# Output projection as seven products of half-size blocks instead of eight, with some of its sums of weights made by accumulating DMAs

## The chip, the core and the metric

One NeuronCore of a Trainium2 chip runs the whole layer. The metric is the device time of one execution in microseconds (us). The engines are TensorE (PE, its weight loads PEld), VectorE (DVE), ScalarE (ACT), GpSimd (POOL) and SyncE (SP), which issues nearly all DMAs.

## What is computed

A decoder layer for 512 tokens of width 2048 in float32: norm, one input projection, three groups of attention heads (16 heads of width 128), a gate, one output projection, a norm, and the residual. The part that matters here:

```
        y = jnp.concatenate([merge_heads(out_a) * jax.nn.silu(ga),
                             merge_heads(out_b) * jax.nn.silu(gb),
                             merge_heads(out_m) * jax.nn.silu(gm)], axis=-1)
        o = jnp.einsum('bse,ed->bsd', y, w_out[layer])
        x = x + rms_norm(o, g_post[layer])
```

y is 512 x 2048, w_out is 2048 x 2048, and the result o is 512 x 2048.

## The kernel before

Every float32 matrix is split into a high part that TensorE takes exactly (float32r) and a low remainder. ACT writes the high part (`hi`, line 859), DVE subtracts it from the original for the low part (`minus`, line 1208), and `three` (lines 540 to 542) issues three matmuls: high x high, low x high, high x low.

**Input projection.** `product(p, i)` works on 28 pairs of column strips. Each pair is done in seven products TOK_A to TOK_G instead of eight, by sums and differences of the halves of tokens and weights (Strassen's way in Winograd's form). Four of the seven take a sum of two weight pieces, added on DVE (line 1237); the split operands go through a ring of three slots, so ACT and DVE work three products ahead of TensorE. The results are combined by small copies and additions in PSUM and SBUF (lines 951, 955, 959, 1325, 1328).

**Output projection.** `out_block(c, p, s)` is plain: for four chunks c of 512 columns, eight pieces p of 256 rows of w_out and four blocks s of 128 tokens, two times three matmuls of 128x128 by 128x512. That is 4 x 8 x 4 x 2 x 3 = 768 matmuls. Eight split buffers hold a whole chunk of w_out, four PSUM banks collect one chunk while the other four are read. y lies in DRAM (`y_dram`), is loaded back by `load_y` one head at a time, and is split by `split_y` (ACT, line 1148) and `lo_y` (DVE). The last head's attention is finished in between: `turn_v`, `turn_probs` and `prob_times_v` (line 688) stand behind pieces 0, 1 and 3 of chunk 0. After each chunk ACT squares and copies its four banks (lines 1178, 1180) and DVE multiplies by the gain g_post (`gpost`, line 1587). In the last chunk the blocks of tokens end one after the other. Each is closed by a root on ACT (line 901), four small DVE steps, four multiply-adds with the residual (line 1611) and four stores (line 529).

**What sets the order.** Every engine has its own queue, written out by hand, with waits on counting semaphores. SP's queue holds all loads in order, so a wait in front of one load holds up every load behind it; `gpost` (line 520) is loaded once the whole of y is split. POOL issues no DMA.

## Time and profile before

| | us |
|---|---|
| median of 3 runs | 936.09 (935.10 to 938.37) |
| profiled execution, its own time | 936.1 |
| its span in the profile | 934.3 |
| end of the input projection on TensorE | 741.65 |
| first matmul of the output projection | 746.48 |
| TensorE, share of the span busy | 97% |
| DVE / ACT, share of the span busy | 70% / 51% |

The time of an execution is 1.8 us more than the span. Start times in the profile are counted from the start of the span. An instruction's duration overlaps its neighbours' a little, so the distance between two starts, and not the duration, tells how fast an engine gets through a row of like instructions.

### The profile page before, as it was taken

How to read it: one execution, taken by the hardware profiler on the slowest of the kernel's cores; microseconds unless marked ns; L12 is line 12 of the kernel's file. 1: busy time of each engine (PE TensorE's matmuls, PEld its weight loads, DVE VectorE, ACT ScalarE, POOL GpSimd, SP SyncE). 2: the span in 40 equal slices, each digit the busy share in tenths (PEclk: the TensorE clock that was granted, in tenths of full speed). 3: DMA queues.
4: the chain of work that ended last, by engine and by line, in shares of the span. 5: the costliest groups of instructions: out<-in, count | busy, mean ns of one | idle time of the engine just before them, and what ended most of it. 6: DMA issues, size and time to landing. Idle time of an engine off the chain costs nothing.

```text
span 934.3 us, 16316 instructions
## 1 busy us (share of the span) xinstructions
PE 901.8 (97%) x6619; PEld 856.4 (92%) x6619; DVE 649.8 (70%) x940; ACT 474.3 (51%) x862; POOL 79.0 (8%) x71
## 2 busy tenths in 40 slices
PE   8997998999999999999999999999999799999996
PEld 5887998999999999999999999999999788888885
DVE  4889978888777777777777777777777653532324
ACT  5786555555545455555555554546464552541311
POOL 0000508600000000000020201011110000000000
PEclk9999999999999999999999999999999999999999
DMA  9951424343334333343434352525252717632016
GB/s 301 290 137 46 127 78 102 102 115 102 102 102 103 102 102 102 103 105 99 114 91 120 85 136 72 148 66 145 70 136 82 260 65 284 234 91 68 0 47 224
DMA packets 155312, 113.42 MB, mean 121 GB/s; under 512 B 6041, under 2 KB 137145, under 8 KB 154086
## 3 DMA queue, kind: packets, MB, share of 16 engines
q1 hardware_dynamic: 154950, 111.34, 41.9%
q8 instruction: 52, 0.85, 0.4%
q10 hardware_dynamic: 288, 1.05, 0.4%
q14 instruction: 22, 0.18, 0.1%
HBM read 104.22 MB, written 9.73 MB: 122 GB/s over the span
## 4 chain that ended last, share of the span: by engine, by line
PE 81%; DVE 10%; ACT 4%; issue 3%; DVEq 0%; POOL 0%; ACTq 0%; POOLq 0%
PE d_ps L540 12%; PE d_ps L542 12%; PE d_ps L541 12%; PE e_ps L540 6%; PE e_ps L542 6%; PE e_ps L541 6%; PE c_ps L540 3%; PE c_ps L542 3%; PE c_ps L541 3%; PE pt_ps L688 3%; DVE ring L1208 3%; PE score_ps L541 2%; PE score_ps L540 2%; PE score_ps L542 2%; DVE sums L1237 2%
## 5 line engine op out<-in xcount | busy, mean ns | idle before, releaser
L1208 DVE TENSOR_TENSOR ring<-sums,ring 128x1024 fp32r<-128x1024 f32 x112 | 140.4, 1255 | 95.7 <-ACT ring L859 95.0
L540 PE MATMUL d_ps<-tok_hi,ring 128*128 128x256 f32 x672 | 191.2, 285 | 2.9 <-DVE ring L1208 2.9
L542 PE MATMUL d_ps<-tok_lo,ring 128*128 128x256 f32 x672 | 190.1, 283 | 0.0
L541 PE MATMUL d_ps<-tok_hi,ring 128*128 128x256 f32 x672 | 190.1, 283 | 0.0
L1208 DVE TENSOR_TENSOR ring<-raw,ring 128x1024 fp32r<-128x1024 f32 x100 | 124.5, 1249 | 45.2 <-ACT ring L859 45.2
L540 PEld LDWEIGHTS d_ps<-tok_hi,ring 128*128 128x128 f32 x672 | 128.9, 192 | 3.3 <-issue 3.3
L859 ACT ACTIVATE ring<-sums 128x1024 fp32r<-128x1024 f32 x112 | 117.9, 1052 | 22.0 <-DVE sums L1237 20.4
L541 PEld LDWEIGHTS d_ps<-tok_hi,ring 128*128 128x128 f32 x672 | 129.0, 192 | 0.0
L542 PEld LDWEIGHTS d_ps<-tok_lo,ring 128*128 128x128 f32 x672 | 128.9, 192 | 0.0
L859 ACT ACTIVATE ring<-raw 128x1024 fp32r<-128x1024 f32 x100 | 105.2, 1058 | 37.5 <-PE d_ps L542 37.5
L1208 DVE TENSOR_TENSOR wout_split<-raw,wout_split 128x1024 fp32r<-128x1024 f32 x32 | 39.1, 1224 | 71.8 <-ACT wout_split L859 71.2
L1237 DVE TENSOR_TENSOR sums<-sums,raw 128x1024 f32<-128x1024 f32 x56 | 69.9, 1248 | 0.0
L1237 DVE TENSOR_TENSOR sums<-raw 128x1024 f32<-128x1024 f32 x56 | 69.8, 1246 | 0.1
L859 ACT ACTIVATE wout_split<-raw 128x1024 fp32r<-128x1024 f32 x32 | 33.8, 1061 | 69.4 <-PE e_ps L542 29.6
L540 PE MATMUL c_ps<-tok,ring 128*128 128x256 f32 x224 | 64.5, 288 | 0.1
L540 PE MATMUL e_ps<-tok_hi,ring 128*128 128x256 f32 x224 | 64.3, 287 | 0.0
L540 PE MATMUL e_ps<-tok,ring 128*128 128x256 f32 x224 | 64.3, 287 | 0.0
L542 PE MATMUL e_ps<-tok_lo,ring 128*128 128x256 f32 x224 | 63.4, 283 | 0.0
L542 PE MATMUL d_ps<-tok,ring 128*128 128x256 f32 x224 | 63.4, 283 | 0.0
L541 PE MATMUL d_ps<-tok,ring 128*128 128x256 f32 x224 | 63.4, 283 | 0.0
L542 PE MATMUL c_ps<-tok,ring 128*128 128x256 f32 x224 | 63.4, 283 | 0.0
L540 PE MATMUL d_ps<-tok,ring 128*128 128x256 f32 x224 | 63.4, 283 | 0.0
(279 smaller groups left out, 2281.0 us busy)
## 6 DMA issues: line engine op xcount, KB each, us to landing
raw<-in_w_in_dram SPq DMA_DIRECT2D x112, 512.0 KB, 5.5
raw<-in_w_out_dram SPq DMA_DIRECT2D x32, 512.0 KB, 5.6
raw<-in_w_mem_kv_dram SPq DMA_DIRECT2D x16, 512.0 KB, 8.3
stage<-in_x_dram SPq DMA_DIRECT2D x4, 1024.0 KB, 9.2
xres<-in_x_dram SPq DMA_DIRECT2D x4, 1024.0 KB, 8.3
out_dram<-o_sb SPq DMA_DIRECT2D x16, 256.0 KB, 3.3
y_dram<-ybuf SPq DMA_DIRECT2D x15, 256.0 KB, 2.3
y_f<-y_dram SPq DMA_DIRECT2D x15, 256.0 KB, 5.2
```

The lines of the kernel that those rows point to most:

```text
L540: pe.matmul(dst, lhs[0], rhs[0], start=start, stop=False, skip_group_check=True)
L541: pe.matmul(dst, lhs[1], rhs[0], start=False, stop=False, skip_group_check=True)
L542: return pe.matmul(dst, lhs[0], rhs[1], start=False, stop=stop, skip_group_check=True)
L688: last = pe.matmul(bank[:, first:S], v, pT[:, hl_p, kb, first:S] if not head.memory else pT_mem[:, hl_p, kb, first:S], start=(hl_v, hl_p, ...
L859: act.activation(dst, src, ACTF.Copy).then_inc(hi_done, 1)
L1208: return dve.tensor_tensor(dst, a_, hi_.bitcast(F32), ALU.subtract)
L1237: dve.tensor_tensor(sum_tile(p, s), one, two, ALU.add).then_inc(sum_done, 1)
```

## The change

The output projection now is done like the input projection. The columns go in two groups g of 1024, the rows of w_out and of y in two halves, the tokens in two halves of 256, and each group is seven products (g, TOK_A) to (g, TOK_G). A product is four steps j (two row tiles of 128 each), a step is 2 x 2 x 3 = 12 matmuls of 128x128 by 128x512. There are 2 x 7 x 4 = 56 steps, in the order of `STEPS`. TOK_A and TOK_D of both groups, which need no sum of weights and no sum of y, stand first as steps 0 to 15; then come B, C, E, F, G of group 0 (steps 16 to 35) and of group 1 (36 to 55).

Split weights go through the same ring of three slots of one step each. ACT and DVE run a loop over the steps: at n they split step n+3, and ACT may begin that when TensorE has done step n. Sums of weights (TOK_B, C, E, F, four pieces each and group: eight sets) are made one step earlier still on DVE (`add_out`), except for three sets, (0, B), (0, F) and (1, F), where a DMA issued by POOL adds a piece of w_out from DRAM onto a tile in SBUF (`add_piece`). y is loaded from DRAM in its quarters (`load_y`), and four sums and differences of quarters (`add_y`, 128x2048) and the splits (`hi_y`, `lo_y`, 128x2048) are spread over n = 0 to 19. PSUM results are combined in `out_taken`; the result of A in negated form is the start value ("seed") of D's banks. The gain is now applied from PSUM or from the combined tile (`gain`), with no copy; `finish` closes the blocks of tokens in the order 2, 3, 0, 1, all four behind the split of the last piece. In the last product, (1, G), the steps run once for each of its two token blocks.

```diff
+OUT_PRODUCTS = [(0, TOK_A), (0, TOK_D), (1, TOK_A), (1, TOK_D)] + [
+    (g, i) for g in range(OUT_GROUPS) for i in (TOK_B, TOK_C, TOK_E, TOK_F, TOK_G)]
+STEPS = [(g, i, j) for g, i in OUT_PRODUCTS for j in ((0, 2, 3, 1) if (g, i) == (0, TOK_D) else range(SUBS))]
+STEP_OF = {step: n for n, step in enumerate(STEPS)}
+ADDED_BY_DMA = [(0, TOK_B), (0, TOK_F), (1, TOK_F)]
...
+RAW_USES = [(g, i) for g, i in OUT_PRODUCTS
+            if i in (TOK_D, TOK_G) or (g, i) == (1, TOK_A) or i in (TOK_B, TOK_E, TOK_F) and (g, i) not in ADDED_BY_DMA]
+OUT_PART = {TOK_A: (0, 0), TOK_B: (1, 1), TOK_D: (0, 1), TOK_E: (1, 0), TOK_F: (0, 1), TOK_G: (1, 1)}
...
+            def load_piece(g, i, j):
+                use = RAW_USES.index((g, i))
+                if use == 0:
+                    sp.wait_ge(lo_done, operand(last_pair, TOK_G) + 1)
+                else:
+                    h, k = RAW_USES[use - 1]
+                    if k in (TOK_A, TOK_D, TOK_G):
+                        sp.wait_ge(lo_done, out_operand((h, k, j)) + 1)
+                    else:
+                        sp.wait_ge(sum_done, out_sum_count((h, k, j)))
+                sp.dma_start(as_rows(raw[:, j]), w_out_piece(g, *OUT_PART[i], j)).then_inc(piece_landed[j], 16)
...
+            load_piece(1, TOK_A, 0)
+            load_y(TOK_F)
+            load_piece(1, TOK_A, 2)
+            load_piece(1, TOK_A, 3)
+            load_piece(1, TOK_A, 1)
+            load_y(TOK_G)
+
+            def load_pieces(g, i):
+                if (g, i) in RAW_USES:
+                    for j in range(SUBS):
+                        load_piece(g, i, j)
+
+            for j in range(SUBS):
+                load_other(0, j)
+            load_pieces(1, TOK_D)
+            sp.wait_ge(y_raw, NH)
             sp.dma_start(gpost[:], g_post.partition_broadcast(P)[:, 0, :]).then_inc(gpost_landed, 16)
...
-            def out_block(c, p, s):
-                e0 = out_e0(p)
-                w = wout_split[p][:].rearrange("p h (j n) -> p h j n", j=2)
-                for j in range(2):
-                    tok_cols = slice(P * s, P * (s + 1))
-                    last = three(out_ps[c % 2][s][:], (y_hi[:, e0 + j, tok_cols], y_lo[:, e0 + j, tok_cols]),
-                                 (w[:, 0, j], w[:, 1, j]), p == 0 and j == 0, p == OPC - 1 and j == 1)
...
+            def out_passes(g, i, j, b, bank):
+
+                w = out_slot((g, i, j)).rearrange("p h (e n) -> p h e n", e=2)
+                hi, lo = token_operand(i)
+                cols = slice(P * b, P * (b + 1))
+                for e in range(2):
+                    k = 2 * j + e
+                    last = three(bank[b][:], (hi[:, k, cols], lo[:, k, cols]), (w[:, 0, e], w[:, 1, e]),
+                                 i in (TOK_A, TOK_B) and k == 0, k == KH - 1)
                 return last
 
...
+                if i == TOK_A and g == 1:
+                    pe.wait_ge(y_raw, NH)
+                    pe.wait_ge(v_ready, last_head.v + 1)
+                if i == TOK_B and g == 1:
+                    pe.wait_ge(o_gained, result_count(0, TOK_F, 1))
+                if i in (TOK_D, TOK_C):
+                    pe.wait_ge(out_seeded, 2 * (g + 1))
+                if i == TOK_E:
+                    pe.wait_ge(out_six_taken, 2 * (g + 1))
+                if i == TOK_F:
+                    pe.wait_ge(out_less_six, 2 * (g + 1))
+                if i == TOK_G:
+                    pe.wait_ge(out_last, 2 * (g + 1))
+
...
+                if n == 3:
+                    pe.wait_ge(pt_ready, last_head.pt + 3)
+                    for b in range(2):
+                        pe.matmul(out_c[b][:], pT[:, 0, 0, 0:P], pT[:, 0, 0], start=True, stop=True
...
+                elif (g, i) in ADDED_BY_DMA:
+                    act.wait_ge((first_added if i == TOK_E else other_added)[j], added_count(g, i))
                 else:
-                    act.wait_ge(o_done, QB * c)
-                hi(out_operand(c, p), wout_split[p][:, 0], raw_tile(m))
+                    act.wait_ge(sum_done, out_sum_count(step))
+                if step == STEPS[-1]:
+                    act.wait_ge(lo_done, out_operand((g, TOK_F, 1)) + 1)
...
-            def copy_out(c, s):
-                act.wait_ge(o_done, QB * c + s + 1)
-                bank = out_ps[c % 2][s]
-                if c + s:
-                    act.wait_ge(part_done, QB * c + s)
-                act.activation(waste_o[:], bank[:], ACTF.Square, accum_out=part[:, s:s + 1]
-                               ).then_inc(part_done, 1)
-                act.activation(o_sb[:, s, S * c:S * (c + 1)], bank[:], ACTF.Copy).then_inc(o_copied, 1)
...
+            def out_taken(g, i):
+
+                if i == TOK_A:
+                    act.wait_ge(used, product_end(g, i))
+                    if g == 0:
+                        act.wait_ge(bank_marked, 2)
+                    else:
+                        act.wait_ge(o_gained, result_count(g - 1, TOK_D, 1))
+                    for b in range(2):
+                        act.activation(out_c[b][:], out_d[g][b][:], ACTF.Copy, scale=-1.0).then_inc(out_seeded, 1)
...
+            for n, (g, i, j) in enumerate(STEPS):
+                if n >= LAST_STEPS:
+                    continue
+                if n % SUBS == 0 and n > 0:
+                    out_taken(*STEPS[n - 1][:2])
+                hi_out(STEPS[n + RING])
+                y_work(n)
...
+            def add_out(step):
+
+                g, i, j = step
+                if step not in OUT_SUMS:
...
+                if n == 6:
+                    dve.wait_ge(y_landed[TOK_B], 16)
+                    dve.wait_ge(y_landed[TOK_E], 16)
+                    add_y(TOK_B, TOK_B, TOK_E, ALU.subtract)
+                if n == 8:
+                    dve.wait_ge(y_landed[TOK_F], 32)
+                    dve.wait_ge(y_raw, NH)
+                    dve.wait_ge(y_sum, 1)
+                    add_y(TOK_C, TOK_B, TOK_F, ALU.add)
+                if n == 9:
+                    dve.wait_ge(y_sum, 2)
+                    lo_y(TOK_B, 5).then_inc(y_ready, 1)
+                if n == 10:
+                    dve.wait_ge(y_landed[TOK_G], 32)
+                    add_y(TOK_G, TOK_G, TOK_C, ALU.subtract)
+                if n == 11:
+                    dve.wait_ge(y_sum, 3)
+                    lo_y(TOK_C, 6).then_inc(y_ready, 1)
...
+            def gain(g, i, b):
+
+                count = result_count(g, i, b)
+                _, _, s, n = results[count - 1]
+                dve.wait_ge(part_done, count)
+                if count == 1:
+                    dve.wait_ge(gpost_landed, 16)
+                o = result_tile(s, n)
+                src = o if i == TOK_E else result_bank(g, i, b)[:]
+                dve.tensor_tensor(o, src, gpost[:, S * n:S * (n + 1)], ALU.mult).then_inc(o_gained, 1)
...
+            for n, (g, i, j) in enumerate(STEPS):
+                if n >= LAST_STEPS:
+                    continue
+                if n % SUBS == 0 and n > 0:
+                    out_taken(*STEPS[n - 1][:2])
+                if n + RING + 1 < len(STEPS):
+                    add_out(STEPS[n + RING + 1])
+                lo_out(STEPS[n + RING])
+                y_work(n)
+                if n % SUBS == 1 and n > 1 and STEPS[n - 2][1] in (TOK_D, TOK_E, TOK_F, TOK_G):
+                    gain(*STEPS[n - 2][:2], 0)
+                    gain(*STEPS[n - 2][:2], 1)
+            lo_out(STEPS[-1])
...
+            def finish(m, s, before):
+
+                dve.wait_ge(part_done, len(results) - 2 + max(m - 1, 0))
+                dve.tensor_reduce(sq[:, s:s + 1], part[:, s], AX_X, ALU.add).then_inc(ssq_done, 1)
+                dve.wait_ge(ssq_done, m + 1)
+                rstd(TILES + m, s, before)
+                dve.wait_ge(xres_landed[s], 16)
+                for j in range(OCH):
+                    o = result_tile(s, j)
+                    dve.wait_ge(o_gained, [r[2:] for r in results].index((s, j)) + 1)
+                    dve.scalar_tensor_tensor(out=o, in0=o, scalar=stat[:, 4, s:s + 1], in1=xres[s][:, S * j:S * (j + 1)],
+                                             op0=ALU.mult, op1=ALU.add).then_inc(final_done, 1)
+
...
+            def add_piece(g, i, j):
+
+                tile, added = (first_w, first_added) if i == TOK_E else (other_w, other_added)
+                if i == TOK_B:
+                    pool.wait_ge(other_landed[j], 16 * (g + 1))
+                elif i == TOK_E:
+                    pool.wait_ge(sum_done, out_sum_count((g, TOK_C, j)))
+                else:
+                    pool.wait_ge(lo_done, out_operand((g, TOK_C, j)) + 1)
+                pool.dma_start(as_rows(tile[j]), w_out_piece(g, *OUT_PART[i], j), accum_op=ALU.add).then_inc(added[j], 16)
+
+            for g, i in ADDED_BY_DMA:
+                for j in range(SUBS):
+                    add_piece(g, i, j)
```

**DVE where the input projection ends.** Before, the words are: `wout_split` the split of a piece of w_out, `y_lo` the low part of a head of y, `rinv` a reciprocal of the last head:

```order
L1208 TENSOR_TENSOR wout_split_103<-raw,wout_split_103 128x1024 [waits hi_done]
L1399 RECIPROCAL rinv<-rowsum 128x2 [waits exp_done]
L1208 TENSOR_TENSOR wout_split_104<-raw,wout_split_104 128x1024 [waits hi_done]
L1354 SCALAR_TENSOR_TENSOR gate<-gate,d_ps 128x256 [waits gate_tanh]
L1208 TENSOR_TENSOR y_lo<-y_f_101,y_hi 128x1024 [waits y_split] x2
```

The changed kernel at the same place, where `ring` is a split weight operand, `tok<-whole_f_100` the low part of y's quarter A and `sums` the first pieces of w_out:

```order
L1418 TENSOR_TENSOR ring<-sums,ring 128x1024 [waits hi_done]
L1777 SCALAR_TENSOR_TENSOR tok<-whole_f_100,tok 128x2048 [waits y_split]
L1627 RECIPROCAL rinv<-rowsum 128x2 [waits exp_done]
L1418 TENSOR_TENSOR ring<-sums,ring 128x1024 [waits hi_done]
L1582 SCALAR_TENSOR_TENSOR gate<-gate,d_ps 128x256 [waits gate_tanh]
```

The low part of y that the first output matmul needs has moved ahead of the last gate and of one split.

**DVE while y is split.** Before, behind the splits of chunk 0, with the last head's part of y (`ybuf`):

```order
L1208 TENSOR_TENSOR y_lo<-y_f_101,y_hi 128x1024 [waits y_split]
L1208 TENSOR_TENSOR wout_split_110<-raw,wout_split_110 128x1024 [waits hi_done]
L1208 TENSOR_TENSOR y_lo<-y_f_101,y_hi 128x512 [waits y_split]
L1317 SCALAR_TENSOR_TENSOR ybuf<-pt_ps,gate 128x512 [waits y_stored,gate_ready,pv_done]
L1208 TENSOR_TENSOR y_lo<-ybuf,y_hi 128x512 [waits y_split]
L1589 MEMSET sq 128x8
L1208 TENSOR_TENSOR wout_split_103<-raw,wout_split_103 128x1024 [waits hi_done,stat_step]
```

The changed kernel at n = 8 to 11 (steps 8 to 11 are product (1, A); `tok_f_86` are quarters of y and their sums, `o_sb_109<-score_ps,gpost` is the gain of (0, D), out of the two banks that (1, D) uses next):

```order
L1418 TENSOR_TENSOR ring<-raw,ring 128x1024 [waits hi_done] x2
L1782 TENSOR_TENSOR tok_f_86<-tok_f_86,whole_f_100 128x2048 [waits y_sum,y_raw,y_landed5]
L1418 TENSOR_TENSOR ring<-raw,ring 128x1024 [waits hi_done]
L1418 TENSOR_TENSOR tok_lo<-tok_f_86,tok_hi 128x2048 [waits y_split,y_sum]
L1841 TENSOR_TENSOR o_sb_109<-score_ps,gpost 128x512 [waits gpost_landed,part_done]
L1841 TENSOR_TENSOR o_sb_109<-score_ps,gpost 128x512 [waits part_done]
L1418 TENSOR_TENSOR ring<-raw,ring 128x1024 [waits hi_done]
L1782 TENSOR_TENSOR tok_f_86<-tok_f_86 128x2048 [waits y_landed6]
L1418 TENSOR_TENSOR ring<-raw,ring 128x1024 [waits hi_done]
L1418 TENSOR_TENSOR tok_lo<-tok_f_86,tok_hi 128x2048 [waits y_split,y_sum]
```

Before, DVE had nothing between the splits of the later chunks but small sums and the gains of a finished chunk; now four of these rows are 2048 elements long, and the gains stand behind two of them. On PE the first matmul of (1, D) waits for `out_seeded`, and ACT writes those seeds once (1, A) is done and both gains are made (`out_taken` in the diff).

**SP's queue around the load of the gain**, before:

```order
L509 DMA y_f_101<-y_dram 128x512
L442 DMA raw<-in_w_out_dram 128x2x512 [waits lo_done]
L520 DMA gpost<-in_g_post_dram 128x2048 [waits y_ready]
L522 DMA xres<-in_x_dram 128x2048 x2
L442 DMA raw<-in_w_out_dram 128x2x512 [waits lo_done] x24
```

and in the changed kernel, where the four `L580` loads are the tiles onto which POOL's DMAs add, and the four `L592` behind them are the pieces of (1, D):

```order
L598 DMA tok_f_86<-y_dram 128x3x256 [waits used]
L598 DMA tok_f_86<-y_dram 128x4x256
L580 DMA raw<-in_w_out_dram 128x2x512 [waits sum_done] x2
L580 DMA other_w_102<-in_w_out_dram 128x2x512 [waits negmax_ready,scores_done]
L580 DMA other_w_103<-in_w_out_dram 128x2x512 [waits negmax_ready,scores_done]
L592 DMA raw<-in_w_out_dram 128x2x512 [waits lo_done] x4
L629 DMA gpost<-in_g_post_dram 128x2048 [waits y_raw]
L592 DMA raw<-in_w_out_dram 128x2x512 [waits lo_done] x4
```

The gain is now loaded behind the pieces of (1, D), each of which waits for the split of a step of (1, A).

## Rows read from the trace of the kernel before

**Rows 1.** The page: the span, and busy time of each engine with its share.
```profile
span 934.3 us, 16316 instructions
...
PE 901.8 (97%) x6619; PEld 856.4 (92%) x6619; DVE 649.8 (70%) x940; ACT 474.3 (51%) x862; POOL 79.0 (8%) x71
```

**Rows 2.** Windows: stretch, length, busy PE, PEld, DVE, ACT, POOL, granted clock, DMA share, GB/s.
```profile
741.65:746.48 4.83, 0.00 (x1) 0.03 (x1) 2.93 (x4) 4.33 (x6) 0.00 (x0) 1.00 1.05 400
746.48:750.20 3.72, 3.72 (x10) 2.90 (x10) 0.99 (x1) 0.00 (x0) 0.00 (x0) 0.54 1.05 385
750.20:926.00 175.80, 175.52 (x783) 145.17 (x781) 68.44 (x99) 57.48 (x90) 0.00 (x0) 1.00 0.35 122
80.00:88.00 8.00, 4.61 (x38) 4.17 (x38) 8.00 (x14) 4.49 (x6) 0.00 (x0) 1.00 0.00 0
```

**Rows 3.** Timeline of PE: start, duration, line, what, and idle time before it.
```profile
746.48 0.54 PE L540 MATMUL d_ps<-wout_split,y_hi 128*128 128x512 f32 x1 [4.83 <-DVE y_lo L1208]
...
750.20 0.40 PE L540 MATMUL d_ps<-wout_split,y_hi 128*128 128x512 f32 x1
...
765.38 0.39 PE L541 MATMUL e_ps<-wout_split,y_lo 128*128 128x512 f32 x1
...
767.42 0.39 PE L541 MATMUL d_ps<-wout_split,y_lo 128*128 128x512 f32 x1
...
771.27 2.03 PE L688 MATMUL pt_ps<-pT,kv 128*128 128x512 f32 x12
```

**Rows 4.** Timeline of DVE at the start of the output projection.
```profile
740.17 1.23 DVE L1208 TENSOR_TENSOR wout_split<-raw,wout_split 128x1024 fp32r<-128x1024 f32 x1 [2.84 <-ACT wout_split L859]
...
764.39 1.22 DVE L1208 TENSOR_TENSOR wout_split<-raw,wout_split 128x1024 fp32r<-128x1024 f32 x1
765.53 1.22 DVE L1208 TENSOR_TENSOR y_lo<-y_f,y_hi 128x1024 fp32r<-128x1024 f32 x1
```

**Rows 5.** ACT's and DVE's instructions on 128x2048, by line: shortest/median/longest ns.
```profile
L941 ACT ACTIVATE tok_hi<-tok_f x4: 1906/1912/1917, 84.7 to 91.6; 128x2048 fp32r<-128x2048 f32 x4
...
L1474 DVE TENSOR_TENSOR tok_f<-tok_f x1: 2270/2270/2270, 87.5 to 87.5; 128x2048 f32<-128x2048 f32 x1
```

**Rows 6.** Timeline of ACT behind the first chunk: a split, a square, a copy, a square.
```profile
796.74 1.06 ACT L859 ACTIVATE wout_split<-raw 128x1024 fp32r<-128x1024 f32 x1 [0.26 <-DMA raw<-in_w_out_dram]
797.71 0.58 ACT L1178 ACTIVATE waste_o<-d_ps 128x512 f32<-128x512 f32 x1
...
798.28 0.59 ACT L1180 ACTIVATE o_sb<-d_ps 128x512 f32<-128x512 f32 x1
798.75 0.60 ACT L1178 ACTIVATE waste_o<-d_ps 128x512 f32<-128x512 f32 x1
```

**Rows 7.** The page's DMA issues: KB each, median us from issue to landing.
```profile
gpost<-in_g_post_dram SPq DMA_DIRECT2D x1, 1024.0 KB, 4.6
```

**Rows 8.** Line 442, pieces of w_out issued between 815 and 835 us: time to landing.
```profile
DMA to landing us min/median/max: 3.7/3.7/3.8
```

**Rows 9.** Timeline of DVE where it closes the token blocks.
```profile
906.34 2.74 DVE L1611 SCALAR_TENSOR_TENSOR o_sb<-o_sb,stat,xres 128x512 f32<-128x512 f32 x4
909.00 0.16 DVE L1581 TENSOR_TENSOR sq<-sq,part 128x1 f32<-128x1 f32 x1
...
909.26 0.68 DVE L1587 TENSOR_TENSOR o_sb<-o_sb,gpost 128x512 f32<-128x512 f32 x1
909.86 0.16 DVE L1255 RECIPROCAL stat<-stat 128x1 f32<-128x1 f32 x1
...
910.68 2.75 DVE L1611 SCALAR_TENSOR_TENSOR o_sb<-o_sb,stat,xres 128x512 f32<-128x512 f32 x4
...
928.45 2.74 DVE L1611 SCALAR_TENSOR_TENSOR o_sb<-o_sb,stat,xres 128x512 f32<-128x512 f32 x4
```

**Rows 10.** Timeline of the last matmul and of ACT's square behind it.
```profile
925.33 0.39 PE L542 MATMUL pt_ps<-wout_split,y_hi 128*128 128x512 f32 x1
...
925.81 0.60 ACT L1178 ACTIVATE waste_o<-pt_ps 128x512 f32<-128x512 f32 x1 [9.52 <-issue]
```

548 lines of the change are left out of this document (337 added, 211 removed).

## The prediction, made before the changed kernel ran

> **What bounds the kernel now.** I read the page first: TensorE is busy for 97% of a span of 934.3 us [rows 1]. Then the windows of the output projection [rows 2]. From 741.65 to 746.48 TensorE does nothing, as it waits for the first low part of y; then 3.72 us run at a granted clock of 0.54, which is the 1.2 GHz level; the rest is busy throughout at 1.00, the 2.4 GHz level. DVE is busy there for 68.4 of 175.8 us, ACT for 57.5. So this stage is TensorE's. A step goes from one matmul to the next in (767.42 - 765.38) / 9 = 0.227 us [rows 3], and 768 of them make 174.1 us. The stage ends with the last matmul, and 8.6 us later the span ends [rows 10]. Taking matmuls away helps only as long as ACT, DVE and the loads keep up with the new order. That is the question here.
>
> **The matmuls.** 56 steps of 12 are 672, so 96 fewer: 96 x 0.227 = **-21.8 us**. A step takes 2.72 us. This term is certain; all others say what comes back.
>
> **The start.** ACT ends the split of step 1 at 740.1, as it does with a piece of w_out now, which DVE takes up at 740.17 [rows 4]; DVE splits it until 741.3, then makes y's low part of 128x2048. Such an instruction takes 2.27 us, 2.2 from start to start [rows 5]. TensorE starts at about 743.7 instead of 746.48: **-2.8**. It has then idled for 2.0 us. A gap of 2.4 us, in the stretch 80 to 88, left the clock at 1.00, and the one of 4.83 did not [rows 2], so I drop the slow matmuls too: nine took 750.20 - 746.48 = 3.72 us [rows 3] for 9 x 0.227, **-1.7**. The half step that waits for the last gate costs +0.3, since two splits stand before that gate on DVE, and two extra matmuls that mark banks +0.5 and their issue; I put **+0.9** for all. The last head's work (`prob_times_v`, 2.0 us, 1.9 of them without overlap [rows 3]) stays as it is.
>
> **The seam from (1, A) to (1, D).** Step 12 must wait for its seeds. I follow the queues, in us from the start of the span. Steps 0 to 3 end at 756.0 (four times 2.72, 0.3, and 1.1 for turning blocks), the marks and the last head end at 758.5, step 4 at 761.2, step 6 at 766.7, steps 7, 8 and 11 at 769.4, 772.1 and 780.3. A split takes 0.97 on ACT [rows 6] and 1.14 on DVE [rows 4] from start to start. ACT begins 0.25 after the moment at which a next matmul would have started, 925.33 + 0.227 [rows 10].
> Step 7 is split at 763.6, 2.4 after step 4. Only then may the piece for step 9 be loaded into its slot; with 3.8 to landing [rows 8] it is there at 768.0 and split at 770.2. The sum of two quarters of y on DVE ends at 772.2, its high part on ACT (1.9 us [rows 5]) at 774.2, the two squares of (0, D) (2 x 0.57 [rows 6]) at 775.3, and step 11 is split by 777.5. SP's queue holds the last piece of (1, D) for that, and the gain behind it, which is issued at about 778.
> Meanwhile DVE makes the next sum (779.7), splits step 12 (780.8) and makes the low part of y's B (783.0). Then it needs the gain. The load took 4.6 us [rows 7], so it would be there at 782.6 if the DMA engines were free. From 763.6 SP issues nine pieces (4.7 MB), a quarter of y (0.9) and the gain (1.05), and POOL four accumulating DMAs of 0.52 MB. The DMA engines moved 385 to 400 GB/s when their share was full [rows 2]. SP's 6.7 MB need 17 us, until 781, and keep nobody waiting. With POOL's 2.1 MB counted as moved once it is 8.8 MB and 22.7 us, until 786.3. No row shows an accumulating DMA: its cost lies between nothing (it would run in the others' gaps) and twice its bytes (two streams in), and nearest are the plain loads of the same 512 KB, so I take it once. Then the two gains (0.6 each [rows 9]) end at 787.6, two seeds at 788.7, and TensorE goes on at 788.9: **+8.6**, and a clock that has fallen as before, **+1.7**. With the gain there in time it is 785.5 and +5.2; with twice the bytes 791.7 for the gain and +14.0.
> The Trainium skill ("DMA: Bandwidth & Descriptors", "Issuing engines are not separate DMA queues") says that transfers of all issuers run on the same 16 DMA engines and interleave. That speaks against this change and for 786.3; no row here shows it, since POOL issued no DMA, and without it the gain would come at 782.6. The same page ("SDMA does more than copy") has the add done by a unit that reduces two streams, which speaks for the double count.
>
> **The seams from C to E.** (g, E) uses the banks of (g, C), which ACT must copy first: 0.25, one split 0.97, a copy 0.47 and the second copy's own 0.6 [rows 6], together 2.3 after the end of C. In group 0 the split itself waits for its sum on DVE, 0.4 more. In the input projection D stands between the two and hides this; here nothing does: 2.3 + 2.7 = **+5.0**. Idle times of this size did not touch the clock [rows 2]. The other seams have a product between.
>
> **DVE's arrears in group 0.** From 787.6 on DVE has, up to the split of step 23, 11 splits and 5 sums of weights at 1.14, six instructions at 2.2 for y and two gains: 18.2 + 13.2 + 1.2 = 32.6, and 1.9 of waiting for ACT, which makes y's high parts before its next split; until 822.1. TensorE would want that step at 788.9 + 1.7 + 11 x 2.72 = 820.5. With a smaller wait at step 21 I take **+2.0**, and expect none in group 1, where DVE has no work for y.
>
> **The tail.** Now the token blocks end one by one and DVE waits for each; the last matmul is followed by 8.6 us. In the changed kernel all four `finish` come behind product (1, F). After its end ACT takes 0.25, two splits, two squares (3.5 with the handing over), DVE a split, a sum and a gain (to 5.7), four small steps 0.82 and four multiply-adds 909.00 - 906.34 = 2.66: 9.2. Each further block costs 910.68 - 909.00 + 2.66 = 4.34 [rows 9], three of them 13.0; the last multiply-add ends at 931.1 [rows 9] and the span at 934.3, 3.2. Together 25.4 after (1, F), of which the last product covers 4 x 2.72 = 10.9. That leaves 14.5 for 8.6: **+5.9**. The table for the root loads beside DVE's split and costs nothing.
>
> **Sum.** -21.8 - 2.8 - 1.7 + 0.9 + 8.6 + 1.7 + 5.0 + 2.0 + 5.9 = -2.2. The profiled execution took 936.1 (span 934.3), the median 936.09, so there is nothing to shift: 936.1 - 2.2 = **933.9 us**. A gain of 21.8 on the matmuls is nearly all given back at four places. Within 0.3%, or 2.8 us, a measurement here can't be told from no change.
>
> **Rivals.**
> *The gain lands in time* (POOL's DMAs find room, or are cheap). The seam costs 5.2 for 8.6: 930.5. For it: the stage moves far less than the engines can, 122 GB/s on average [rows 2], and SP's own bytes are through by 781. Against: they are crowded in just these 20 us.
> *ACT and DVE keep closer to TensorE than my sum of queues has it*, as where the work on y at n = 6 to 9 starts earlier. If the seam costs 4 or less, the clock holds as well, and the arrears go: 933.9 - 4.6 - 1.7 - 1 = 926.6 to 929. For it: ACT is busy for only a third of this stage. Against: each wait in my chain is written in the queues.
> *Slower: an accumulating DMA takes the engines for twice its bytes.* The gain lands at 791.7, the seam costs 14.0 for 8.6: 939.3; at three times it is 945. It decides from where the gain lands after some 791: then 5 us are added and the time is over 938.9. For it: the add reads its target too. Against: nothing in the trace shows the rate.
>
> **How the numbers follow.** Forecast within 0.3%, 933.9, its own range 933.3 to 938.9: chance 0.36. Gain in time, 930.5: 0.26. Closer queues, 927 to 929: 0.12. Accumulation twice or more, 939 to 945: 0.26. So faster 0.38, same 0.36, slower 0.26. The range for 8 in 10 must reach into both sides: 928 (half of the third case left out) to 943 (the three-fold DMA left out).
>
> **What would show it.** 672 matmuls of 512 columns at 0.227; TensorE's first of them near 743.7, with the clock at 1.00. The longest wait of the stage at the first matmul of (1, D), with ACT's seed as releaser and, before it, DVE's gain waiting for the DMA of `gpost`; a window at the lower clock behind it. Waits of 2 to 3 us at the first matmul of E in both groups. Some 14 to 15 us from the last matmul to the end, DVE busy throughout. It is wrong if the seeds are made before 784, if POOL's DMAs land late enough that ACT waits for them in (0, B), which I expect to be covered by at least 5 us, or if DVE's contention with POOL stretches its 1.14 us.

## The result, and the profile after

The changed kernel takes 938.93 us (median of 20 runs, 936.03 to 940.98), the kernel before beside it 935.66 (934.22 to 938.37): the ratio is 1.0029, with a 95% interval of 1.002 to 1.0038. The forecast was 933.9 us, a gain of 0.24%; it is a loss of 0.29%. The profiled execution took 941.0 us, 2.1 over the median. An execution can run at a lower clock throughout, and the one such slow run among the variants below (1111.24 us at a granted clock of 0.725, with the sums of (0, B) by DVE) is left out of its median.

The page of the changed kernel, to be read beside [rows 1]; its last line is the queue of the pool engine's accumulating transfers:

```profile
span 939.2 us, 16252 instructions
...
PE 888.9 (95%) x6525; PEld 842.7 (90%) x6525; DVE 717.4 (76%) x985; ACT 503.4 (54%) x882; POOL 92.4 (10%) x83
...
q0 software_dynamic: 3264, 6.29, 4.1%
```

TensorE has 94 matmuls fewer (96 fewer and the two that mark banks) and DVE 67.6 us more work. The windows (stretch, length, busy PE, PEld, DVE, ACT, POOL, granted clock, DMA share, GB/s) answer [rows 2]:

```profile
741.00:746.00 5.00, 2.99 (x22) 2.64 (x22) 4.50 (x5) 4.06 (x9) 0.00 (x0) 1.00 1.07 368
783.40:792.40 9.00, 0.09 (x2) 0.00 (x1) 5.07 (x6) 4.87 (x5) 1.23 (x1) 0.79 0.96 315
792.40:796.00 3.60, 3.60 (x9) 2.85 (x10) 3.60 (x3) 0.00 (x0) 1.20 (x1) 0.57 0.63 155
832.00:836.00 4.00, 4.00 (x13) 3.13 (x13) 2.23 (x3) 0.00 (x0) 1.22 (x1) 0.63 0.99 351
890.00:894.00 4.00, 3.76 (x11) 2.96 (x12) 1.69 (x3) 0.19 (x1) 1.20 (x1) 0.64 1.06 414
...
745.15:925.61 180.46, 163.27 (x696) 131.79 (x697) 130.74 (x134) 86.56 (x111) 14.64 (x12) 0.96 0.71 211
```

The start is short and at the full clock, as forecast. The nine us before 792.40 are the seam from (1, A) to (1, D). Then come three stretches at about 0.6, where one was forecast: the clock is at its 1.2 GHz level behind the seam, and again behind both pauses from C to E. The last row is the whole stage: 0.71 for the share of the DMA engines, which was 0.35 before, and a DVE with 130.7 us of work where it had 68.4.

The seam in the timeline (start, duration, engine, line, what, idle time before it and what ended it):

```profile
780.86 0.73 SPq L629 DMA_DIRECT2D gpost<-in_g_post_dram  x1
...
789.89 1.29 DVE L1841 TENSOR_TENSOR o_sb<-score_ps,gpost 128x512 f32<-128x512 f32 x2 [3.93 <-DMA gpost<-in_g_post_dram]
...
791.27 1.07 ACT L1345 ACTIVATE score_ps<-pt_ps 128x512 f32<-128x512 f32 x2 [3.50 <-DVE o_sb L1841]
...
792.40 0.79 PE L664 MATMUL score_ps<-ring,tok 128*128 128x512 f32 x1 [8.91 <-ACT score_ps L1345]
792.99 0.63 PE L665 MATMUL score_ps<-ring,tok 128*128 128x512 f32 x1
```

Read from below: TensorE waits for ACT's seeds, ACT for DVE's gain, DVE for the load of the gain vector, which takes 8.9 us where it took 4.6 before [rows 7]. The chain is the one that the prediction names. What else TensorE and ACT wait for in the stage, from the list of waits (who waits, for whom, us in total, times, longest):

```profile
PE score_ps L664 <- ACT score_ps L1345: 8.9, 1, 8.9
ACT ring L1009 <- DMA raw<-in_w_out_dram: 6.9, 3, 3.2
...
PE d_ps L664 <- issue: 2.5, 1, 2.5
PE pt_ps L664 <- ACT out_six L1359: 2.2, 1, 2.2
...
PE d_ps L664 <- DVE ring L1418: 1.9, 2, 1.0
PE pt_ps L664 <- DVE ring L1418: 1.1, 1, 1.1
ACT ring L1009 <- DMA other_w<-in_w_out_dram: 1.1, 1, 1.1
```

The end of the program, to be read beside [rows 9, 10]: DVE's first and last four multiply-adds, and the last matmul.

```profile
920.45 2.74 DVE L1895 SCALAR_TENSOR_TENSOR o_sb<-o_sb,stat,xres 128x512 f32<-128x512 f32 x4
...
925.61 0.39 PE L666 MATMUL pt_ps<-extra,tok_hi 128*128 128x512 f32 x1
...
933.46 2.74 DVE L1895 SCALAR_TENSOR_TENSOR o_sb<-o_sb,stat,xres 128x512 f32<-128x512 f32 x4
```

From the last matmul's end (926.0) to the span's end it is 13.2 us, and DVE is busy throughout.

In the account below a step goes from the start of one matmul of 512 columns to the start of the next, and what it takes over 0.227 us is lost. A step of over 0.5 us is a pause; a slow step takes 0.3 to 0.5 us, 0.43 at the lower clock and 0.34 right behind a pause. From the first matmul of the stage to the last the changed kernel loses 18.7 us in pauses and 5.6 us in slow steps.

### The profile page after: what moved, and what is told of

Same layout as the page of the kernel before. It is cut to its first block, busy times and chain, and to the rows that moved or that the text cites. A ratio compares the mean times of both kernels' runs of the same rounds, so it can differ in the third digit from the quotient of the medians.

```text
span 939.2 us, 16252 instructions
## 1 busy us (share of the span) xinstructions
PE 888.9 (95%) x6525; PEld 842.7 (90%) x6525; DVE 717.4 (76%) x985; ACT 503.4 (54%) x882; POOL 92.4 (10%) x83
## 3 DMA queue, kind: packets, MB, share of 16 engines
q0 software_dynamic: 3264, 6.29, 4.1%
## 4 chain that ended last, share of the span: by engine, by line
PE 76%; DVE 13%; ACT 5%; issue 4%; DMA 1%; DVEq 0%; POOL 0%; SPq 0%; ACTq 0%; POOLq 0%
PE d_ps L664 12%; PE d_ps L666 12%; PE d_ps L665 12%; PE e_ps L664 6%; PE e_ps L666 6%; PE e_ps L665 6%; DVE ring L1418 3%; PE c_ps L664 3%; PE c_ps L666 3%; PE c_ps L665 3%; PE pt_ps L811 3%; ACT ring L1009 2%; PE score_ps L664 2%; PE score_ps L665 1%; PE score_ps L666 1%
## 5 line engine op out<-in xcount | busy, mean ns | idle before, releaser
L1418 DVE TENSOR_TENSOR ring<-sums,ring 128x1024 fp32r<-128x1024 f32 x121 | 151.9, 1256 | 98.7 <-ACT ring L1009 98.2
L1418 DVE TENSOR_TENSOR ring<-raw,ring 128x1024 fp32r<-128x1024 f32 x131 | 162.0, 1239 | 68.9 <-ACT ring L1009 68.6
L1009 ACT ACTIVATE ring<-raw 128x1024 fp32r<-128x1024 f32 x131 | 138.0, 1058 | 78.3 <-PE d_ps L666 47.6
L1009 ACT ACTIVATE ring<-sums 128x1024 fp32r<-128x1024 f32 x121 | 127.4, 1053 | 31.1 <-DVE sums L1445 17.7
L664 PE MATMUL e_ps<-tok_hi,ring 128*128 128x256 f32 x224 | 64.3, 287 | 0.0
L664 PE MATMUL e_ps<-tok,ring 128*128 128x256 f32 x224 | 64.3, 287 | 0.0
L666 PE MATMUL e_ps<-tok,ring 128*128 128x256 f32 x224 | 63.4, 283 | 0.0
L665 PE MATMUL e_ps<-tok_hi,ring 128*128 128x256 f32 x224 | 63.4, 283 | 0.0
```

Source lines behind the costliest of these rows:

```text
L664: pe.matmul(dst, lhs[0], rhs[0], start=start, stop=False, skip_group_check=True)
L665: pe.matmul(dst, lhs[1], rhs[0], start=False, stop=False, skip_group_check=True)
L666: return pe.matmul(dst, lhs[0], rhs[1], start=False, stop=stop, skip_group_check=True)
L1009: act.activation(dst, src, ACTF.Copy).then_inc(hi_done, 1)
L1418: return dve.tensor_tensor(dst, a_, hi_.bitcast(F32), ALU.subtract)
```

## The experiments

All variants are edits of the changed kernel. Each was measured against the kernel before on the same chip; ratios are to it.

### The changed kernel again

> The changed kernel again, unaltered, so that the variants beside it have it on the same chip. Both theories: 938.9 us, 1.0029 of before. In the profile the wait of TensorE between the third and the fourth product is 8.9 us (last matmul at 783.1, first at 792.4), both pauses between C and E are 2.3 to 2.6 us, and whether the clock falls after each of the three pauses of that size (before E's predecessor at 93, and the two at 829 and 888) shows whether that is chance.

939.48 us, ratio 1.0039 (1.0024 to 1.0053). The seam's pause is 9.3 us, the two from C to E 2.65 and 2.34, and the clock falls behind both. The whole stage lies 1.45 us earlier than in the first profile, and that comes from long before the change: 0.4 us from before 17 us, and 1.0 from behind 92, where the clock fell in the first profile and not in the repetition. In these two windows the program is the same. The changed kernel's first profile:

```profile
90.00:94.00 4.00, 1.56 (x9) 1.16 (x7) 4.00 (x5) 4.00 (x4) 0.00 (x0) 0.80 0.00 0
```

The repetition:

```profile
90.00:94.00 4.00, 1.61 (x13) 1.55 (x14) 4.00 (x4) 3.59 (x2) 0.00 (x0) 1.00 0.02 4
```

So comparisons of one profile with another are made inside the stage, from its own first matmul.

### The seam: place or bytes?

My theory was that the gain vector comes late because it stands behind four pieces of weights in SP's queue.

```
+            sp.wait_ge(y_raw, NH)
+            sp.dma_start(gpost[:], g_post...)      # ahead
             load_pieces(1, TOK_D)
-            sp.wait_ge(y_raw, NH)
-            sp.dma_start(gpost[:], g_post...)
```

> The load of the gain vector (1 MB) is issued ahead of the four pieces for the product (group 1, D) instead of behind them: at about 769 instead of 780.9 us. Nothing else changes. Theory 1 (the seam before (1,D) is set by this load's place in SyncE's queue): it lands at about 779 to 781, the gain runs at 786 right behind the split of B's low part, the seeds at 787.3, the first matmul at 788.5 instead of 792.4: 3.5 to 4 us less, 935.0 to 935.4 us, ratio to before 0.9990 to 0.9995. Rival (the transfers as a whole are the limit: 1 MB put in front pushes the four pieces back by the same 2.7 us): the piece for step 12, which ScalarE already waits for until 783.98, lands at about 786.7, its split ends at about 789 and the product starts at 789 to 790: 2.4 to 3.3 us less, and further waits of ScalarE on the pieces behind it.

939.47 us, ratio 1.0039 (1.0025 to 1.0052): nothing. The theory fell. The timeline of ACT and DVE:

```profile
783.85 1.06 ACT L1009 ACTIVATE ring<-raw 128x1024 fp32r<-128x1024 f32 x1 [6.78 <-DMA raw<-in_w_out_dram]
...
788.28 1.28 DVE L1841 TENSOR_TENSOR o_sb<-score_ps,gpost 128x512 f32<-128x512 f32 x2
```

The gain waits for no load any more. But ACT now waits 6.8 us for the first piece of (1, D), and with it all that stands behind that split on ACT and DVE; TensorE's pause is 9.5 us. One late transfer was exchanged for another.

The next run takes DVE's order away as well: the gains one loop earlier.

```
                 lo_out(STEPS[n + RING])
+                if n == 2 * SUBS:
+                    gain(0, TOK_D, 0)
+                    gain(0, TOK_D, 1)
                 y_work(n)
```

> As the run with the early load of the gain vector, and the two gains of (0,D) are made one loop earlier on VectorE, ahead of the sum for C's tokens and of the split of B's low part. Theory 1 (order of VectorE): gains at about 780.4, seeds as soon as (1,A) ends at 783.1, first matmul of (1,D) at 784.5 to 786.0, TensorE's pause 1.5 to 3 us instead of 9.1, and the matmuls behind it at the full clock: 6 to 8 us less than the changed kernel, 931 to 933 us. Rival (the pieces' transfers decide): the pause stays at 6 to 7 us since the split of step 12 is only made at 788 to 789: 935 to 936.5 us, no better than the run with the early load alone.

937.63 us, ratio 1.0017 (1.0005 to 1.003). The pause is 8.8 us. The gain is made at 781.06, ACT ends the late splits only at 789.6 and makes the seeds then. That the run is nearly 2 us faster has, in its profile, another reason: the clock stays at 1.00 behind both pauses from C to E (below).

Then the bytes. The gains of (0, D) read a quarter of the vector, 256 KB:

```
+            load_gain(0)                  # columns 0 to 511
             load_pieces(1, TOK_D)
+            for n in range(1, OCH):
+                load_gain(n)
```

> The load of the gain vector (1 MB) in four quarters of 256 KB: the first, all that the gains of (0,D) read, ahead of the four pieces for (group 1, D), the other three behind them. After the run with the whole load in front (its gain was ready, but the pieces landed 6 us later and the seam stayed at 9.5 us) the theory is that the bytes in front decide. Theory 1 (bytes in the queue): the first quarter lands before 782, the pieces land 0.7 to 1.6 us later than in the changed kernel, the gain runs at about 785, the seeds at 786.3, the first matmul of (1,D) at 787.5 instead of 791.0 in the changed kernel's profile: 3 to 4 us less, 935 to 936 us. Rival (any load in front of the pieces delays them as much as the 1 MB did, by the queue's order and not by its bytes): the seam stays at 9 to 9.5 us, 939 us.

936.75 us, ratio 1.002 (1.0009 to 1.0032). The pause is 7.0 us, the first matmul of (1, D) at 788.83: 2.3 us less, where 3 to 4 were expected. So the bytes in front matter, and not the place as such. In this profile the clock falls behind only one of the two pauses from C to E.

Last, the quarter, the earlier gains, and the pieces of (1, D) ahead of three of four pieces that only the accumulations of (0, B) need:

```
             load_other(0, 0)
+            load_gain(0)
+            load_piece(1, TOK_D, 0)
+            load_piece(1, TOK_D, 1)
+            load_other(0, 1)
+            load_piece(1, TOK_D, 2)
+            load_other(0, 2)
+            load_piece(1, TOK_D, 3)
+            load_other(0, 3)
```

> The quarter in front as in the run before, the two gains of (0,D) one loop earlier on VectorE, and the pieces for (1,D) issued ahead of three of the four pieces that only the accumulating transfers of (0,B) need (those are issued one behind each piece of (1,D)). Theory 1 (the seam is the sum of a queue of transfers and VectorE's order, both now out of the way): pieces at 776 to 781, gain at about 779, seeds at 783 to 785, pause of TensorE 2.5 to 4.5 us instead of 9.5: 5 to 7 us less, 932 to 934 us, below before. Rival (the accumulating transfers, which now start later since their plain halves do, become late for (0,B) at 803): ScalarE waits for them there and TensorE loses what it won, 936 to 939 us.

936.46 us, ratio 1.0008 (0.9996 to 1.0021). The pause is 4.35 us, five less, and the first matmul of (1, D) comes 4.8 us earlier than in the repeated changed kernel, counted from the stage's own first matmul. The rest is seen in ACT's queue: the high part of C's tokens until 784.6, a split until 785.6, and only then the seeds. The median shows less of it: one pause in (0, C) grew from 1.1 to 1.9 us, and this kernel's runs spread from 933.0 to 939.5.

### What the accumulating transfers do

> The sums of the product (group 0, B) made by VectorE (four additions of about 1.22 us) from plain loads, instead of by four accumulating transfers; the sums of both F stay as they are. The plain loads are 4 x 512 KB, as many bytes as before. Theory 1 (the accumulating transfers are cheap for the engines, and VectorE has no room in these loops): the sums come at loops 12 to 15 of VectorE, which is late by 3.5 us in this stage already: 2 to 5 us more, 941 to 944 us, with new pauses between steps 16 and 19. Rival (the accumulating transfers are what makes the pieces for (1,D) and the gain vector late, because they take the transfer engines for much longer than plain ones): the seam shortens by 2 us or more and the total is 936 to 938 us.

```
-ADDED_BY_DMA = [(0, TOK_B), (0, TOK_F), (1, TOK_F)]
+ADDED_BY_DMA = [(0, TOK_F), (1, TOK_F)]
```

940.18 us, ratio 1.0047 (1.0035 to 1.0059). Both theories have a part: the gain vector lands 2 us earlier and the seam's pause is 7.1 us instead of 9.3, so the transfers do stand in its way; and 0.8 us more are lost in (0, C), 1.5 before a step of (1, F). By the ratios, accumulating by DMA there is worth 0.7 to 1.7 us to this kernel in all, with intervals that overlap.

In the changed kernel's first profile the pool engine issues one such transfer and then pauses, without waiting for anything named (timeline of POOL):

```profile
774.55 1.34 POOL L1964 DMA_DIRECT2D raw<-in_w_out_dram  x1 [71.17 <-DMA raw<-in_w_out_dram]
785.26 1.23 POOL L1964 DMA_DIRECT2D raw<-in_w_out_dram  x1 [9.36 <-issue]
793.88 1.20 POOL L1964 DMA_DIRECT2D other_w<-in_w_out_dram  x1 [7.40 <-issue]
```

Each goes out 0.3 us after the one before has landed (785.00 and 793.62). The next run doubles the memory for descriptors, `dynamic_dma_scratch_size=1024` to 2048.

> The descriptor memory of the pool engine's own transfers is doubled from 1024 to 2048 bytes per partition; nothing else changes. Theory 1 (with 1024 only one accumulating transfer fits at a time, which is why the pool engine pauses 5.6 to 9.3 us between two issues without waiting for anything that the trace names): the second transfer of each set is issued as soon as its plain half is there, within 2 us of the first, idle time put down to issue falls from 29 us to under 10, and the total hardly moves, 938 to 939 us, since ScalarE waited for such a transfer for only 1.1 us. Rival (the pool engine writes its descriptors slowly or waits for the transfer's end whatever the memory): the same pauses.

943.21 us, ratio 1.0079 (1.0066 to 1.0092). The first half of my theory holds, as the timeline of the pool engine and DVE shows:

```profile
773.00 2.59 POOL L1964 DMA_DIRECT2D raw<-in_w_out_dram  x2 [70.84 <-DMA raw<-in_w_out_dram]
775.67 1.19 POOL L1964 DMA_DIRECT2D other_w<-in_w_out_dram  x1
783.70 1.22 POOL L1964 DMA_DIRECT2D other_w<-in_w_out_dram  x1 [6.84 <-issue]
...
793.37 1.29 DVE L1841 TENSOR_TENSOR o_sb<-score_ps,gpost 128x512 f32<-128x512 f32 x2 [8.99 <-DMA gpost<-in_g_post_dram]
```

Three are issued within 4 us, which the small memory had spread over 19. The second half is wrong by 4 us: these transfers now move in just the time in which the gain vector is on its way, it lands 4.8 us later, and the pause before (1, D) grows from 9.3 to 14.1 us. The small memory had, by chance, kept them out of the way. The medians of the two kernels are 3.7 us apart.

The Trainium skill ("DMA: Bandwidth & Descriptors", "Issuing engines are not separate DMA queues") has the transfers of all issuers share the 16 engines; these two runs agree, with 2.2 us won without the pool engine's transfers and 4.8 lost with more of them in flight.

> The twelve transfers of the pool engine copy instead of accumulate: the second part of the weights replaces the first instead of being added, so that sum is left out of the computation; their number, sizes, queue and waits stay the same. Theory 1 (accumulating costs the transfer engines 2.3 times as much per byte as copying): from issue to landing 8 to 10 us become 4 to 6, the shares of the 16 engines for this queue 4.1 becomes about 1.8 per cent, pieces for (1,D) land 1 to 2 us earlier, and the total is 936.5 to 938 us. Rival (it is the queue that is driven by the pool engine, and not the addition, that makes them slow): landing times and total unchanged.

```
-  pool.dma_start(..., accum_op=ALU.add)
+  pool.dma_start(...)
```

This variant leaves the sum out, so its result is not the layer's. 938.5 us, ratio 1.0037 (1.0019 to 1.0055). Five of its seven runs took 937.9 to 938.9 us and two 942.6 and 943.9; the profile is of the one at 942.6. The queue's line on the page, which was 3264 packets and 4.1%:

```profile
q0 software_dynamic: 1728, 6.29, 1.9%
```

The same bytes take the engines for less than half the time, so the forecast of the share was right: adding costs some 2.1 times a copy (4.1% for 1.9%). The forecast of the seam did not hold in the profiled execution. With about half the packets each, three transfers are issued within 3.4 us, the gain vector comes later (gain at 791.52) and the pause is 12.7 us. Against the changed kernel the run doesn't give the price of the addition, because the times of issue moved with it. Against the kernel with doubled memory it nearly does, as the first three transfers are issued at the same times there (772.9, 774.2, 775.6 for 773.0, 774.3, 775.7): the pause is 12.7 us for 14.1, the profiled executions are 1.1 us apart and the medians 4.7. What the engines moved while the seam built up:

```profile
763.00:767.00 4.00, 4.00 (x19) 3.33 (x18) 3.19 (x6) 1.36 (x2) 0.00 (x0) 1.00 0.53 101
...
763.00:789.00 26.00, 17.68 (x77) 14.00 (x75) 14.65 (x13) 12.48 (x14) 3.13 (x4) 0.90 0.96 340
```

### The clock behind a pause

Between C and E stand, in both groups, nine matmuls that nobody reads:

```
                 if i == TOK_E:
+                    pe.wait_ge(o_gained, result_count(1, TOK_D, 1))
+                    hi, _ = token_operand(TOK_D)
+                    for k in range(9):
+                        pe.matmul(out_c[0][:], hi[:, 0, 0:P], hi[:, 0:2], start=True, stop=True)
                     pe.wait_ge(out_six_taken, 2 * (g + 1))
```

> Nine extra matmuls of 512 columns into a bank that nobody reads any more, between C and E of both groups, where TensorE waits for ScalarE's copies: they add 9 x 0.227 = 2.04 us of work inside pauses of 2.62 and 2.33 us. Nothing that the output depends on changes. Theory 1 (the pause makes the clock fall, which costs 1.6 us behind each): the pauses stay as long, no matmul after them is spaced at 0.43 us, the granted clock stays at 1.00 at 832 to 836 and at 890 to 894: 3.2 us less, 935.7 us, ratio 0.9995 to before. Rival (the clock falls for another reason, or falls anyway at this point of the run): 938.9 us or up to 0.5 more.

938.42 us, ratio 1.003 (1.0017 to 1.0043). A window behind the first seam from C to E, in the repeated changed kernel:

```profile
830.60:836.00 5.40, 5.40 (x17) 4.31 (x18) 2.49 (x5) 1.06 (x1) 1.22 (x1) 0.68 0.91 299
```

With fillers:

```profile
830.60:836.00 5.40, 4.99 (x22) 3.79 (x22) 3.69 (x6) 2.08 (x4) 0.34 (x1) 1.00 1.03 289
```

The same stretch of the kernel with fillers in the timeline of TensorE:

```profile
829.05 2.20 PE L954 MATMUL score_ps<-tok 128*128 128x512 f32 x9
831.67 0.50 PE L664 MATMUL d_ps<-ring,tok_hi 128*128 128x512 f32 x1 [0.41 <-ACT out_six L1363]
```

The pause is as long, filled, and no matmul behind it runs at the lower clock: inside the stage 2.6 us of slow steps are left of 5.7. But 1.5 us come back as a pause before a step of (1, F), whose accumulated weights were not there for the earlier date, and in this profile the clock had fallen at 90 to 94 us again. The median has only 0.5 to 1.1 us of the gain, with intervals that overlap. Inside the stage it is 1.95 us, from 180.59 to 178.64 between first and last matmul. The clean test came later, with those weights early: the combined kernel, with and without the fillers.

> As the combined kernel with F at 24 and G at 29 and 2048 bytes, without the nine filler matmuls at each seam from C to E. Theory 1 (the clock falls behind a pause of 2.3 to 2.6 us in most executions, 1.6 us each time, and not where fillers stand in the pause): 2 to 3.2 us more than with them, 930.5 to 932.5 us, and a wider spread from run to run. Rival (the fillers do nothing, the clock falls elsewhere instead): the same time within 1 us.

930.53 us (929.33 to 930.86) without, 927.29 (926.56 to 929.24) with: 3.2 us, two times 1.6. The 13 profiles without fillers (the changed kernel twice) have 26 pauses from C to E, of 2.3 to 2.7 us, and the clock falls behind 19 of them: behind both in eight profiles, behind one in three, behind none in two, and the pauses where it falls are no longer than those where it doesn't. Behind the 12 such seams with fillers it never falls. So the length of such a pause does not decide whether the clock falls behind it.

Places ahead of the output projection say the same. There the twenty profiles (one of the kernel before, nineteen of the changed kernel and its variants) have equal idle times to 0.03 us. Behind the idle time of 2.4 us at 82 the clock fell in none of the 20, behind 2.4 us at 92 in 5, behind 2.3 us at 154 in 6, and behind 1.8 us at 33 in 17. Behind the idle time of 2.0 us ahead of the stage's first matmul it fell in 3 of the 19 profiles of the changed kernel and its variants. At 92 it came out both ways in one and the same program, the changed kernel. What decides it stays open.

The trace of before could have warned. Besides the pause in the stretch from 80 to 88 [rows 2] it has these two, in its timeline of TensorE:

```profile
32.86 0.35 PE L540 MATMUL d_ps<-memT,ring 128*128 128x256 f32 x1 [1.76 <-DVE ring L1208]
...
92.34 0.38 PE L759 MATMUL c_ps<-tok 128*128 128x256 f32 x1 [2.44 <-DVE kmv L1208]
```

and these windows behind them:

```profile
33.40:36.80 3.40, 3.40 (x18) 3.40 (x17) 3.26 (x10) 0.74 (x2) 0.00 (x0) 0.50 1.14 300
92.30:96.30 4.00, 3.96 (x33) 3.88 (x34) 4.00 (x4) 1.82 (x2) 0.00 (x0) 1.00 0.01 4
```

The shorter idle time has the lower clock behind it, the longer one has not.

### DVE's arrears

> The splits of the low parts of the tokens of G and F (2.29 us each on VectorE) are moved from steps 17 and 19 to steps 25 and 26, into (group 0, E), where VectorE has room; G is needed at step 32, F at step 28. Theory 1 (VectorE's arrears in these loops cause the pauses of 1.1 us at 817 and 824): both pauses go, 2.2 us less, and the copies of the sixth partial result and the seam from C to E follow 2.2 us earlier, with the same length: 936.7 us, ratio to before 1.001. Rival (what is late there are the pieces or the accumulated sums): the pauses stay, 938.9 us.

```
-  n == 17: lo_y(TOK_G, 8)      n == 19: lo_y(TOK_F, 9)
+  n == 25: lo_y(TOK_G, 8)      n == 26: lo_y(TOK_F, 9)
```

940.64 us, ratio 1.0048 (1.0035 to 1.0062). The pauses at 817 and 824 are gone. In their place, in the timeline of DVE and TensorE:

```profile
841.80 2.28 DVE L1418 TENSOR_TENSOR tok<-whole_f,tok 128x2048 fp32r<-128x2048 f32 x1
...
844.14 0.50 PE L664 MATMUL c_ps<-ring,tok 128*128 128x512 f32 x1 [2.57 <-DVE tok L1418]
```

F's low part at step 26 is too late for (0, F). The theory was right on the two pauses and wrong on the room. With F at 24 and G at 29:

> The changed kernel with the split of F's low part at step 24 and of G's at step 29 (F is needed at 28, G at 32), instead of at 19 and 17. Theory 1 (the arrears are badly placed work: VectorE is idle for over 1 us a step in (0,E) and (0,F)): the pauses at 817 and 824 go and none comes before (0,F) or (0,G): 2.2 us less, 936.7 us, ratio 1.000 to 1.001. Rival (there is no room: (0,F) or (0,G) start late as (0,F) did with the splits at 25 and 26): 938.5 to 940.5 us.

937.56 us, ratio 1.0021 (1.0012 to 1.003). The two pauses are gone and what comes instead is 0.5 us before G and 1.5 in (1, F), the late accumulated weights again. The work was badly placed, not too much; but it pays in full only when the weights of (1, F) come earlier.

### The last stage

ACT scales and the pool engine adds for two of the four final multiply-adds of the first three row blocks:

```
+  act.activation(o, o, ACTF.Copy, scale=stat[:, 4, s:s + 1])
+  pool.tensor_tensor(o, o, xres[s][:, S * j:S * (j + 1)], ALU.add)
```

> In the last stage, of the four final multiply-adds of each of the first three row blocks, two are done as a scaling by ScalarE and an addition by the pool engine; VectorE keeps two (and all four of the last block). Theory 1 (the chain of VectorE, four blocks of 4.34 us from 918.77, sets the end): the blocks shrink to about 3.0 us, the last multiply-add ends at 932.5 to 933.5 instead of 936.1 and the span is 3 to 4 us shorter: 935 to 936 us. Rival 1 (the last matmul at 926.0 and the last block behind it set the end: no gain beyond 926.0 + 0.4 + 0.7 + 4.3 = 931.4 plus 3.1): same figures as above at best, so not told apart. Rival 2 (the pool engine's additions slow VectorE's down or take over 2 us each, and the stores wait for them): 938 to 941 us.

936.39 us, ratio 1.0011 (0.9999 to 1.0022). A block of DVE takes 3.88 us for 4.34, not 3.0. The reason stands in the timeline of POOL and DVE:

```profile
916.21 2.94 POOL L1993 TENSOR_TENSOR o_sb<-o_sb,xres 128x512 f32<-128x512 f32 x2 [17.20 <-ACT o_sb L1411]
...
918.15 1.02 DVE L1509 TENSOR_TENSOR stat<-stat 128x1 f32<-128x1 f32 x1
```

A DVE instruction on one column, else 0.16 us, lasts 1.02 us and ends at 919.17, when the pool engine's additions end at 919.15; so it does in each of the three blocks. It is the last of the block's small steps; the three just ahead of it, beside the same additions, take their usual 0.15 to 0.22 us, and why this one alone waits stays open. From the first matmul of the last split to the end of the span it is 19.1 us for 20.3: 1.2 won. The rest of the better median is not from here; in this profile, which is 1.6 us under the median, the stage starts 2 us earlier and the clock falls behind neither pause.

### All together

> All that helped, together: the quarter of the gain vector and the pieces of (1,D) ahead of the pieces for (0,B), the gains of (0,D) one loop earlier; on ScalarE the split of step 11 ahead of the squares of (0,D), and the seeds for (1,D) ahead of the high part of C's tokens; the low parts of G and F at steps 25 and 26; the filler matmuls between C and E; the doubled descriptor memory; and in the last stage one of the four final multiply-adds of the first three row blocks as a scaling by ScalarE and an addition by the pool engine. Theory 1 (each pause has the cause found for it, so the gains add): against the changed kernel 8 us at the seam from (1,A) to (1,D) with 1.6 for the clock behind it, 1.2 in (1,A), 2.2 of VectorE's arrears, 3.2 for the clock behind C, 2 at the end: 16 to 18 us, 921 to 924 us, ratio to before 0.984 to 0.988. Rival (every pause that goes lays bare the transfers behind it: pieces and accumulated sums become the limit): half of it, 928 to 932 us.

932.27 us, ratio 0.996 (0.9946 to 0.9974), 7 us less than the changed kernel and under half of what the sum promised: the pause before (1, D) is 1.8 us, but F's low part costs its 2.7 us, steps 13 to 16 and 18 each wait 0.4 to 0.6 us for DVE, and sharing one multiply-add made DVE's block 4.7 us long instead of shorter. Its timeline:

```profile
912.24 3.12 DVE L1940 SCALAR_TENSOR_TENSOR o_sb<-o_sb,stat,xres 128x512 f32<-128x512 f32 x3
...
913.11 1.69 POOL L2020 TENSOR_TENSOR o_sb<-o_sb,xres 128x512 f32<-128x512 f32 x1 [35.48 <-ACT o_sb L1433]
```

Three of these took 3.12 us beside the addition, four take 2.74 alone [rows 9]. In this profile the clock also falls behind the idle time of 2.0 us ahead of the stage's first matmul.

> The combined kernel with F's low part at step 24 and G's at 29. Theory 1: the pause of 2.73 us before (0,F) at 833 and the slow matmuls behind it (1.6) go: 3 to 4.3 us less than the combined kernel's 932.3: 928 to 929.3 us, ratio to before 0.992 to 0.993. Rival (the pause moves to (0,G)): 931 to 933 us.

927.29 us, ratio 0.9913 (0.9901 to 0.9925): 5.0 us less (4.4 by the ratios, as the chip is another), by moving two instructions.

> As the run before, with the descriptor memory of the pool engine's transfers back at 1024 bytes. Theory 1 (accumulating transfers that go out one at a time keep out of the way of the pieces, which matters only where those are late; with them in front it doesn't, and then the late sums of (1,F) cost 1 to 1.7 us): 929 to 931 us, 1 to 2 us more than with 2048. Rival (they still get in the way of the pieces for (1,D) with 2048): 926 to 928 us, less than with 2048.

937.7 us, ratio 1.0019 (1.0004 to 1.0034), 10 us more, where 1 to 2 were expected. The direction was right, the size was not: in (0, B) TensorE waits 1.4 and 3.3 us for sums that were issued one by one at 774.5, 783.4, 793.4 and 802.1, the clock falls behind the longer of the two, and 1.7 us are lost in (1, F). So the same memory costs 4 us in the changed kernel, where the pieces of (1, D) stand behind the loads for the accumulations, and is worth 10 in the combined one, where they stand ahead. The two kernels differ in other edits too, so that it is the order of the pieces which turns the sign is argued and not shown.

> The combined kernel (F's low part at 24, G's at 29, fillers, 2048 bytes) with the last stage as in the changed kernel: all sixteen final multiply-adds on VectorE. Theory 1 (VectorE's blocks set the end; with one of four multiply-adds shared a block took 4.67 us, with none 4.34): 3 x 0.33 = 1.0 us less than the 927.3 us with one shared: 926.3 us. Rival (the last matmul or the stores set the end): 927.3 us as before.

925.49 us, ratio 0.9895 (0.988 to 0.991), the lowest median of all: 1.8 us less than with one multiply-add shared, on another chip and with intervals that overlap. From the last split to the end it is 20.3 us for 21.4, which is the 1.0 us expected. The rest is not from this edit: the stage starts 2.0 us earlier in this profile, and then 1.6 us are lost as the clock falls behind the idle time ahead of its first matmul:

```profile
741.50:745.00 3.50, 3.42 (x8) 2.75 (x9) 1.55 (x4) 1.23 (x2) 0.00 (x0) 0.51 1.07 371
```

> The combined kernel with two of four multiply-adds shared (a scaling by ScalarE, an addition by the pool engine) in the first three row blocks, instead of one. Theory 1 (a block takes 3.88 us, as in the run with this edit alone): 3 x (4.67 - 3.88) = 2.4 us less than with one shared, 924.9 us, and 1.4 us less than with none; ratio to before 0.988. Rival (the last block waits for the last matmul's squares, or the stores queue up behind the pool engine's results): 926.5 to 928 us.

926.93 us, ratio 0.9902 (0.9886 to 0.9919). The blocks did shrink to 3.9 us, and from the last split to the end it is 19.2 us for 20.3; but this profile's stage starts 2.4 us later than the other's, before any edit, and four runs each don't separate the two. Whether two shared multiply-adds pay stays open within 1.5 us.

The stage of the fastest kernel as a window, to be held against the last window of the changed kernel above:

```profile
741.58:910.17 168.59, 164.79 (x715) 132.88 (x715) 130.20 (x134) 86.24 (x111) 14.54 (x12) 0.99 0.76 225
```

168.6 us for 180.5, with 18 more matmuls in it, DVE and ACT as busy as before and the clock at 0.99. Pauses are 5.6 us for 18.7, slow steps 2.8 for 5.6. The gain on the matmuls was there all the time; the order gave it back.

## Why the prediction was wrong

By its own steps, in us of the profiles:

| term | forecast | measured |
|---|---|---|
| matmuls | -21.8 | -21.8, spaced at 0.227 |
| start | -2.8 | -2.8 (2.01 idle for 4.83) |
| clock at the start | -1.7 | -1.7 (1.00) |
| seam (1, A) to (1, D) | +8.6 | +9.1 |
| clock behind it | +1.7 | +1.7 |
| C to E, both groups | +5.0 | +5.0 (2.62 and 2.33) |
| clock behind these | 0 | +3.2 |
| DVE's arrears | +2.0 | +3.5 (1.24, 1.07, 1.15) |
| last split | 0 | +0.8 |
| tail | +5.9 | +4.6 (13.2 for 8.6) |
| half step, marks and the rest | +0.9 | +1.8 |
| sum | -2.2 | +3.4 |

The last term is what is left of the measured sum, 196.06 - 192.65 from the end of the input projection to the end of the span; 0.9 of it I can't place. With 1.5 us that the first profile lost before that point it is the difference of the two spans, 4.9.

**The step that failed** is one sentence in "The seams from C to E": "Idle times of this size did not touch the clock". It put the clock behind these two seams at nothing, on the strength of one stretch of one execution. The trace it was taken from has two more pauses of 2.3 to 2.4 us without a fall, at 92 and 154, but also a fall behind an idle time of only 1.76 us at 33, which the prediction left out. In the changed kernel the clock fell behind both seams: seven steps at 0.43 instead of 0.227 and two between cost 1.6 us, twice. The run with fillers showed the effect inside the stage, and the pair of combined kernels, with and without fillers on one chip, its price in the medians, 3.2 us. With this step alone put right the forecast would have been 937.1, slower, and within 0.2% of the result.

**Mis-sized: DVE's arrears**, 3.5 for 2.0. One pause came before the seam, at 780.48, where I had expected none. There I had taken 3.8 us for a piece to land [rows 8]; the one for step 9, issued at 765.52, took 4.85, and those issued behind it, from 767 to 776, took 7.3 to 11.2. So step 9's split, the sum of y's quarters, ACT's squares and step 11's split came 1.1 to 1.5 us later than I had them, counted from the stage's first matmul, one after the other. That the two later pauses are placement was shown by the runs that moved two splits.

**The last split** (0.8) wasn't in the sum: `extra` is split behind two squares on ACT, and TensorE waits for it.

**The tail** was over-sized: the chain of four blocks of 4.34 us was right to the hundredth (918.77, 923.10, 927.44, 931.78), its start was earlier against the last matmul than I had it.

**Right:** the seam with its whole chain and its size. The chain was reasoned, but the size is luck, because errors cancelled. I let POOL's four transfers run close together; they came one at a time, over 28 us, held back by the small descriptor memory. I counted their bytes once; the share of 4.1% for 1.9% as copies says that the engines spent twice the time of a copy on them. And I let the engines move 385 to 400 GB/s from the first piece on. The kernel in which the same transfers are copies and run close together is the case of my single count, and its profile has a pause of 12.7 us, not 8.6: from 763 to 789 it moved 340 GB/s, as the share of the engines was only 0.53 in the first four. By that rate 8.8 MB take 25.9 us instead of 22.7, an estimate that covers 3.2 of the 4.1 us. With the doubled memory the adding ones run together too, and the pause is 14.1 us, near the +14.0 that the prediction gave for twice their bytes. That this too is partly luck follows from the 12.7. That the gain vector's place in SP's queue hardly matters, and the bytes ahead of the pieces do, the prediction did not say. ACT did not wait for POOL's transfers in (0, B), but the last of the four, landed at 807.89 and split at 809.22, was covered by 1.3 us and not by 5.

**Right in part by luck:** the clock at the start. It held behind the 2.0 us of idle time here, and in 16 of the 19 profiles of the changed kernel and its variants; in three it fell.

**The rivals.** The gain in time (930.5) and the closer queues (926.6 to 929) did not come. The last one's trigger, a gain landing after 791, wasn't reached (789.9), though its time of 939.3 was nearly met, for another reason.

## What to carry to other kernels

When matmuls are removed and products moved together, price the pauses between them twice: the pause, and a fall of the clock behind each of some two us, even where one such pause in the old trace left it alone. Take every pause of that trace for the forecast, and not one. A few matmuls without use in the pause are the cheap cure, worth 3.2 us here. Where several transfers are late at one place, changing the order of two of them exchanges one wait for another; send fewer bytes first (the quarter that the next instruction reads), and move what is needed much later behind. And test a resource such as the descriptor memory together with the order: the same doubling cost 4 us in one order and brought 10 in the other.

## What the runs showed of the hardware

- One accumulating transfer of 512 KB at a time with 1024 bytes of descriptor memory, idle times of 5 to 10 us between two issues, and each issue 0.3 us behind the landing of the one before; with 2048 the idle time between the first two is gone. Each issue takes the pool engine 1.2 us (0.73 for a copy), and from issue to landing it is 5.8 to 11.1 us.
- An accumulating transfer takes the DMA engines some 2.1 times as long as a copy of the same bytes (4.1 and 1.9% of the span for 6.29 MB), in 3264 packets for 1728.
- The clock fell behind 19 of 26 pauses of 2.3 to 2.7 us and behind none of 12 that were filled with nine matmuls. The first slow matmul came within 2 us of the pause's end, and seven or eight steps in a row were slow. At other places it fell behind idle times of 1.8 us in 17 of 20 profiles, of 2.0 in 3 of 19, of 2.3 in 6 of 20, and of 2.4 in 5 of 20 at one place and in none at another.
- Beside a pool engine addition of 128x512 (1.5 to 1.7 us each) DVE's three multiply-adds took 3.1 us, where four alone take 2.74. A one-column instruction took 0.85 us longer and ended with the addition, while three others of one column and a multiplication out of PSUM (0.68) took their usual time beside the additions.
